# The fourth mixer of a 1-core block stack: compression inputs from two tiles, rotary halves by transfers

## The reference

```python
q = apply_rope(q, cos, sin) * (HEAD_DIM ** -0.5)      # 8 heads of 64, 2 groups
kc, vc, ks, vs, kw, vw = [groups(z) for z in (kc, vc, ks, vs, kw, vw)]   # 2 groups of 64 each
ks = apply_rope(ks, cos, sin)
kw = apply_rope(kw, cos, sin)
k_cmp = apply_rope(compress_blocks(kc, pe_k, w1_k, w2_k), ccos, csin)
v_cmp = compress_blocks(vc, pe_v, w1_v, w2_v)

def apply_rope(x, cos, sin):
    x1, x2 = jnp.split(x, 2, axis=-1)                 # halves of 32 channels
    rot = jnp.concatenate([-x2, x1], axis=-1)
    return x * cos + rot * sin

def compress_blocks(z, pe, w1, w2):                   # 31 blocks of 32 tokens, one every 16 tokens
    blocks = (z[:, :, idx] + pe).reshape(B, G, n_cmp, CMP_BLOCK * d)     # 2048 inputs a block
    return jax.nn.gelu(blocks @ w1) @ w2
```

## Time and profile before

| | |
|---|---|
| median of 3 runs | 2870.78 us (2868.59 to 2872.48) |
| profiled execution | 2868.78 us, its span 2867.0 us |
| mean granted TensorE clock | 0.963 |
| PE, DVE, ACT, POOL busy | 94%, 53%, 34%, 12% of the span |
| stage 7, from gates to the last attention step | about 2085 to 2450 us |

### The profile page before, as it was taken

One profiled execution on the slowest core, in us unless ns is written; L12 is line 12 of the kernel. 1 busy time (PEld: TensorE's weight loads), 2 busy tenths in 40 slices (PEclk: granted clock), 3 DMA queues, 4 the chain that ended last, 5 costly groups with the idle time before them and its releaser, 6 DMA issues.

```text
span 2867.0 us, 32354 instructions
## 1 busy us (share of the span) xinstructions
PE 2704.0 (94%) x13312; PEld 2142.0 (75%) x13312; DVE 1509.2 (53%) x2062; ACT 986.6 (34%) x1662; POOL 350.5 (12%) x306
## 2 busy tenths in 40 slices
PE   7879998999999988899999999999999977999998
PEld 6767876788888665586788888888878534788886
DVE  7965897544334678546434334343365367543333
ACT  3214654422222533543322223222233335332221
POOL 0001001222200001000222102221000000122200
PEclk9979999999999998799999999999999878999999
DMA  3333112122232221001333332223322200133232
GB/s 137 76 83 127 62 53 70 65 98 99 97 96 93 74 67 47 8 2 61 102 99 100 96 98 94 96 96 100 98 92 96 68 15 1 52 104 100 98 94 83
DMA packets 77539, 229.04 MB, mean 80 GB/s; under 512 B 16976, under 2 KB 18256, under 8 KB 77136
## 3 DMA queue, kind: packets, MB, share of 16 engines
q1 hardware_dynamic: 64464, 213.51, 22.9%
q0 software_dynamic: 1840, 5.77, 1.1%
q10 hardware_dynamic: 11088, 7.70, 0.9%
HBM read 221.18 MB, written 5.77 MB: 79 GB/s over the span
## 4 chain that ended last, share of the span: by engine, by line
PE 79%; DVE 13%; ACT 5%; issue 1%; DMA 1%; ACTq 1%; POOL 0%; DVEq 0%; POOLq 0%
PE ps L354 78%; DVE mem L371 5%; DVE part L441 2%; ACT part L429 1%; PE ps L365 1%; DVE mem L384 1%; DMA mem<-lag_dram 1%; DVE mem L2887 1%; DVE mem L377 1%; DVE ps L371 1%; ACTq L1139 1%; DVE mem L389 1%; DVE mem L549 0%; ACT mem L505 0%; DVE mem L630 0%
## 5 line engine op out<-in xcount | busy, mean ns | idle before, releaser
L354 PE MATMUL ps<-part,part 128*128 128x512 f32 (+2 forms) x9918 | 2277.4, 391 | 41.3 <-DVE part L441 18.2
L354 PEld LDWEIGHTS ps<-part,part 128*128 128x128 f32 x9918 | 1855.1, 189 | 461.1 <-DVE part L441 22.0
L441 DVE TENSOR_TENSOR part<-mem,part 128x1024 fp32r<-128x1024 f32 (+2 forms) x421 | 561.2, 1340 | 579.6 <-ACT part L429 579.1
L429 ACT ACTIVATE part<-mem 128x1024 fp32r<-128x1024 f32 (+2 forms) x421 | 417.5, 1002 | 224.6 <-DMA mem<-in_ffb_down 56.7
L371 DVE TENSOR_TENSOR mem<-ps,mem 128x512 f32<-128x512 f32 (+2 forms) x296 | 195.6, 661 | 345.3 <-PE ps L354 335.7
L354 PE MATMUL ps<-mem 128*64 128x64 f32 (+13 forms) x2568 | 273.1, 317 | 60.3 <-DVE mem L371 29.3
L354 PEld LDWEIGHTS ps<-mem 128*64 128x64 f32 (+4 forms) x2568 | 185.3, 169 | 138.8 <-issue 54.5
L513 POOL TENSOR_TENSOR mem<-mem 128x512 f32<-128x512 f32 x62 | 80.8, 1304 | 1132.5 <-ACT mem L505 1131.5
L1557 ACT ACTIVATE part<-mem 128x512 fp32r<-128x512 f32 x88 | 55.6, 632 | 328.5 <-DVE mem L371 328.5
L371 DVE TENSOR_TENSOR mem<-mem 128x512 f32<-128x512 f32 (+10 forms) x289 | 141.8, 491 | 43.2 <-ACT mem L1584 11.4
L1554 ACT ACTIVATE mem<-mem 128x512 f32<-128x512 f32 x88 | 55.6, 632 | 314.2 <-DVE mem L371 314.2
(11 more groups left out here) (178 smaller groups left out, 1060.8 us busy)
## 6 DMA issues: line engine op xcount, KB each, us to landing
mem<-in_ffa_gate SPq DMA_DIRECT2D x44, 512.0 KB, 3.2
mem<-in_ffa_up SPq DMA_DIRECT2D x44, 512.0 KB, 3.2
mem<-in_ffb_gate SPq DMA_DIRECT2D x44, 512.0 KB, 3.2
mem<-in_ffb_up SPq DMA_DIRECT2D x44, 512.0 KB, 3.2
mem<-in_ffa_down SPq DMA_DIRECT2D x32, 512.0 KB, 3.5
mem<-in_ffb_down SPq DMA_DIRECT2D x32, 512.0 KB, 3.6
mem<-in_w_odd SPq DMA_DIRECT2D x24, 512.0 KB, 3.2
mem<-in_w_ab SPq DMA_DIRECT2D x22, 512.0 KB, 3.2
```

Of the source, the lines that this page charges most:

```text
L354: return e.matmul(out, l, r, start=start, stop=stop, skip_group_check=True)
L429: w.e.activation(K.wts[c % NH].h[:, 0:n], K.raws[c % NR][:, 0:n], ACT.Copy).then_inc(*K_A.up(("w", c)))
L441: w.e.tensor_tensor(t.l, K.raws[c % NR][:, 0:n], t.hf, SUB).then_inc(*K.V.up(("w", c)))
```

## The change

The weights hold kc and vc once (two "blocks" tiles, two groups of 64 channels each), so all later weight numbers fall by two. DVE scales each tile from PSUM into SBUF (`E.kv`). POOL issues two transfers that put its halves the other way about into `E.vk`, copies four pieces from `E.kv` into KCX or VCX, waits for the transfers and copies four from `E.vk`. ACT's casts and DVE's subtractions of the two inputs move into the first two rounds.

For cq and ck no product is made. POOL waits for ACT's copy of the tile and issues four transfers of 32 partitions into `turned` (the buffer that held the product before). DVE multiplies the tile by cos, waits for the transfers, multiplies by sin (the sign is in the table now) and adds; it does so one round later, after the next round's first `weights_lo`. The rotation of the compressed keys (`kcm`) and of the third mixer stays a product, with the sign in the table.

```diff
-    rows("w_cd", range(6, 10))
+    rows("w_cd", range(6, 8))
...
+def turn_gpsimd(K, w, name, o, raw, turned, which):
+    w.wait_ge(*K.A[name, o])
+    for r in range(4):
+        a = 32 * (r ^ 1)
+        w.e.dma_start(turned[32 * r:32 * r + 32, :], raw[a:a + 32, 0:T]).then_inc(
+            *K.counts[f"turned{which}"].up((name, o), by=16))
...
+def turned_vector(K, w, name, o, dst, raw, turned, which, cos, sin):
+    w.wait_ge(*K.A[name, o])
+    w.e.tensor_tensor(dst, raw[:, 0:T], cos, MUL).then_inc(*K.V.up())
+    w.wait_ge(*K.counts[f"turned{which}"][name, o])
+    w.e.tensor_tensor(turned, turned, sin, MUL).then_inc(*K.V.up())
+    tt(w, dst, dst, turned, ADD, (name, "rope", o))
...
 (cd_tensor)
-    for _ in linear(K, w, "blocks", 4, 8, K.h, h_ready, K.V):
+    for _ in linear(K, w, "blocks", 2, 8, K.h, h_ready, K.V):
...
         compress_tensor(K, w, i // 4, i % 4)
-        if i < 4:
-            rope_tensor(K, w, "cq", i, E.rope[i % 2][0], T)
-        elif i < 6:
-            rope_tensor(K, w, "ck", i - 4, E.rope[i % 2][0], T)
...
 (cd_vector)
+    for o in range(2):
         weights_lo(K, w, c + 13 + o + 3)
         w.wait_ge(*K.P["blocks", o])
+        w.e.tensor_tensor(E.kv[o], K.acc("blocks", o), K.rstd, MUL).then_inc(*K.V.up(("blocks", o)))
     for o in range(6):
+        weights_lo(K, w, c + 15 + 2 * o + 3)
+        if o < 2:
+            z = (E.KCX, E.VCX)[o]
+            w.wait_ge(*K.A["CX", o])
+            tt(w, E.CX[o].l, z.rearrange("p j n -> p (j n)"), E.CX[o].hf, SUB, ("CX", o))
         if o == 4:
             compress_vector(K, w, 0)
+        if o == 5:
+            cd_keys_vector(K, w)
+        if o:
+            cd_rope_vector(K, w, o - 1)
+        weights_lo(K, w, c + 15 + 2 * o + 4)
+    cd_rope_vector(K, w, 5)
+    weights_lo(K, w, c + 35)
...
 (cd_scalar)
     for o in range(6):
+        weights_hi(K, w, c + 15 + 2 * o + 3)
+        if o < 2:
+            z = (E.KCX, E.VCX)[o]
+            w.wait_ge(*K.G["blocks", o])
+            e.activation(E.CX[o].h, z.rearrange("p j n -> p (j n)"), ACT.Copy).then_inc(*K.A.up(("CX", o)))
...
 (cd_gpsimd)
+    for o in range(2):
+        blocks_gpsimd(K, w, o)
+    for o in range(6):
+        turn_gpsimd(K, w, "cq" if o < 4 else "ck", o % 4, *E.rope[o % 2], o % 2)
...
+def blocks_gpsimd(K, w, o):
+    E, e = K.cd, w.e
+    z = (E.KCX, E.VCX)[o]
+    w.wait_ge(*K.V["blocks", o])
+    landed = K.counts[f"other{o}"]
+    for half in range(2):
+        e.dma_start(E.vk[o][64 * half:64 * half + 64, :], E.kv[o][64 - 64 * half:128 - 64 * half, :]).then_inc(
+            *landed.up("landed", by=16))
+    for other in range(2):
+        if other:
+            w.wait_ge(*landed["landed"])
+        src = (E.kv, E.vk)[other][o].rearrange("p (n s) -> p s n", s=16)
+        for half in range(2):
+            r, g = slice(64 * half, 64 * half + 64), half ^ other
+            for lo in range(2):
+                copy(w, z[r, 8 * lo:8 * lo + 8, 31 * g:31 * g + 31], src[r, half:16:2, lo:lo + 31], ("blocks", o))
```

More of the change, by code:

```diff
@@ L171, in __init__ @@
         inputs = ("consts", "consts1", "params0", "params", "x0", "x1", "x2", "x3", "x4", "x5", "x6", "x7", "ssm_bc", "pool_w", "w2a2", "g2", "nsa_w2")
-        moved = ["raw0", "raw1", "shuffle", "out", "lag_zeros", "lags_out", "lags_in"]
+        moved = ["raw0", "raw1", "shuffle", "turned0", "turned1", "other0", "other1", "out", "lag_zeros", "lags_out", "lags_in"]
         moved += [f"{n}{tl}" for n in ("u_out", "u_in", "y_out", "y_in") for tl in range(4)]
@@ L333, in weight_order @@
     first[7] = len(out)
-    rows("w_cd", [18])
-    rows("w_cd", range(10, 18))
+    rows("w_cd", [16])
+    rows("w_cd", range(8, 16))
     by_token("w_dv", T)
-    rows("w_cd", range(6, 10))
+    rows("w_cd", range(6, 8))
     nsa = [(io["nsa_w1"][kv, c], 1024, False) for kv in range(2) for c in range(4)]
@@ L2473, in __init__ @@
         self.kk = m.tiles(2)
+        self.kv, self.vk = (self.q[:, 2 + k, :] for k in range(2)), (self.kk[:, k, :] for k in range(2))
+        self.kv, self.vk = list(self.kv), list(self.vk)
         self.vt = m.flat(NT * 280).rearrange("p (t c) -> p t c", t=NT)
@@ L2764, in cd_vector @@
     stt(w, E.sin, K.cc("sin"), 0.125, K.rstd, MUL, MUL)
-    turned = K.rstd.rearrange("p (n s) -> p s n", s=16)
-    for o in range(4):
+    for o in range(2):
         weights_lo(K, w, c + 13 + o + 3)
         w.wait_ge(*K.P["blocks", o])
[L2769 to L2778, removed]
-    for o in range(6):
-        weights_lo(K, w, c + 17 + 2 * o + 3)
+        w.e.tensor_tensor(E.kv[o], K.acc("blocks", o), K.rstd, MUL).then_inc(*K.V.up(("blocks", o)))
+    for o in range(6):
+        weights_lo(K, w, c + 15 + 2 * o + 3)
[3 more added lines that the diff above has]
+            tt(w, E.CX[o].l, z.rearrange("p j n -> p (j n)"), E.CX[o].hf, SUB, ("CX", o))
         if o == 4:
             compress_vector(K, w, 0)
[L2783 to L2788, removed]
+        if o == 5:
[5 more added lines that the diff above has]
+    weights_lo(K, w, c + 35)
     w.wait_ge(*K.A["gates_c"])
@@ L2793, in cd_vector, with cd_keys_vector, cd_rope_vector @@
     mlstm_vector(K, w)
-    weights_lo(K, w, c + 39)
+    weights_lo(K, w, c + 37)
     nsa_vector(K, w)
-    out_vector(K, w, 7, lambda o: c + 35 + o, 8, lambda k: K.pc("ffb_norm", 8 + k))
+    out_vector(K, w, 7, lambda o: c + 33 + o, 8, lambda k: K.pc("ffb_norm", 8 + k))
+def cd_keys_vector(K, w):
+    E = K.cd
+    ts(w, E.cos, E.cos, 8.0, None, MUL, None)
+    ts(w, E.sin, E.sin, 8.0, None, MUL, None)
+    w.wait_ge(*K.V.now)
+def cd_rope_vector(K, w, o):
+    E = K.cd
+    name, dst = ("cq", E.q[:, o, :]) if o < 4 else ("ck", E.kk[:, o - 4, :])
+    turned_vector(K, w, name, o % 4, dst, *E.rope[o % 2], o % 2, E.cos, E.sin)
 def compress_vector(K, w, kv):
@@ L2968, in cd_scalar @@
         e.activation(E.dv[:, t, :], K.acc("dv", t), ACT.Copy, scale=K.rT[:, t:t + 1]).then_inc(*K.A.up(("dv", t)))
-    for o in range(4):
+    for o in range(2):
         weights_hi(K, w, c + 13 + o + 3)
[L2971 to L2974, removed]
     for o in range(6):
-        weights_hi(K, w, c + 17 + 2 * o + 3)
+        weights_hi(K, w, c + 15 + 2 * o + 3)
[3 more added lines that the diff above has]
+            e.activation(E.CX[o].h, z.rearrange("p j n -> p (j n)"), ACT.Copy).then_inc(*K.A.up(("CX", o)))
         if o == 4:
@@ L2982, in cd_scalar @@
         rope_scalar(K, w, name, o % 4, E.rope[o % 2][0], T)
-        weights_hi(K, w, c + 17 + 2 * o + 4)
+        weights_hi(K, w, c + 15 + 2 * o + 4)
     for t in range(4):
-        weights_hi(K, w, c + 29 + t + 3)
+        weights_hi(K, w, c + 27 + t + 3)
     for t in range(4):
@@ L2990, in cd_scalar @@
     e.activation(E.gt, E.vt[:, :, 256:280], ACT.Sigmoid).then_inc(*K.A.up("gates_c"))
-    weights_hi(K, w, c + 37)
+    weights_hi(K, w, c + 35)
     compress_scalar(K, w, 1)
     mlstm_scalar(K, w)
-    weights_hi(K, w, c + 39)
+    weights_hi(K, w, c + 37)
     nsa_scalar(K, w)
-    out_scalar(K, w, 7, lambda o: c + 35 + o, 8, lambda k: K.pc("ffb_norm", 8 + k))
+    out_scalar(K, w, 7, lambda o: c + 33 + o, 8, lambda k: K.pc("ffb_norm", 8 + k))
 def compress_scalar(K, w, kv):
@@ L3117, in cd_gpsimd @@
     memset(w, E.kcd, 0.0, "vcm_zeros")
-    out_gpsimd(K, w, 7, lambda o: K.first[7] + 35 + o, 8)
+    for o in range(2):
+        blocks_gpsimd(K, w, o)
+    for o in range(6):
+        turn_gpsimd(K, w, "cq" if o < 4 else "ck", o % 4, *E.rope[o % 2], o % 2)
+    out_gpsimd(K, w, 7, lambda o: K.first[7] + 33 + o, 8)
+def blocks_gpsimd(K, w, o):
[14 more added lines that the diff above has]
+                copy(w, z[r, 8 * lo:8 * lo + 8, 31 * g:31 * g + 31], src[r, half:16:2, lo:lo + 31], ("blocks", o))
 def sync(K, e):
@@ L3227, in _constants @@
         for d in range(32):
-            R[b + d + 32, b + d] = -1
+            R[b + d + 32, b + d] = 1
             R[b + d, b + d + 32] = 1
@@ L3234, in tabs @@
         ang = pos.astype(f)[None, :] * np.tile(inv, 4)[:, None]
-        return np.cos(ang), np.sin(ang)
+        return np.cos(ang), np.sin(ang) * np.where(i % 64 < 32, -1, 1)[:, None]
     a, b = tabs(np.arange(T))
@@ L3351, in _layout @@
     di, df, dog = cd[:, 2328:2332], cd[:, 2332:2336], cd[:, 2336:2848]
-    dup = [np.concatenate([z[:, 64 * g:64 * g + 64]] * 2, 1) for z in (kc, vc) for g in range(2)]
     ifg = np.zeros((1024, P), f)
@@ L3355, in _layout @@
     ifg[:, 32:36] = df
-    out["w_cd"] = _w(np.concatenate([qc, ks, kw] + dup + [dq, dk, dog, ifg], 1))
+    out["w_cd"] = _w(np.concatenate([qc, ks, kw, kc, vc, dq, dk, dog, ifg], 1))
     out["w_cv"] = np.ascontiguousarray(np.concatenate([vs, vw, cg], 1)).reshape(8, P, 280)
```

## The result

The changed kernel took 2856.72 us (median of 5 runs, 2856.34 to 2862.55); the kernel before, run beside it, 2872.48 (median of 5, 2868.59 to 2879.63). The ratio is 0.9948, with a 95% interval of 0.9936 to 0.9960: faster by 0.4 to 0.6%. The forecast was 2855.1 with a range of 2849.5 to 2863. The execution that was profiled is the slowest of the five, 2862.55 (span 2860.7, mean granted clock 0.959), so its end is not the place to read the gain. I read it between points that both traces have: an eviction, the end of a product.

What follows compares the result with a forecast made beforehand. PE's gapless stretch in the fourth mixer was taken as the bound: 16.3 us removed, 0.6 waited, 0 for rotary transfers and clock, so 15.7 gained and 2855.1 us forecast; 8-in-10 range 2849.5 to 2863.

Steps and rivals of the forecast that it cites:

- PE bounds, gapless: Around the fourth mixer, PE alone is the chain from 2129.63 to 2263.86, so PE work removed there shortens the kernel equally.
- Blocks products, 10.9: Two of the four blocks products leave PE, 2 x 5.45 = 10.9 us.
- B: The end of blocks product 0, at 2168.05 in the trace before; the first input's chain is counted from it.
- Rotations, 0.9 each: Six products with the rotation matrix leave PE's rounds, 0.9 us each, 5.4 us together (3.2 to 6.6).
- The input's chain and its wait, 0.6: Scaling, transfers, eight copies, cast and subtraction delay the first compression input; PE waits 0.6 us, ends 0 and 4.5.
- x: Time in us from one of POOL's strided copies to the next; 0.73 taken first, 0.89 for the wait of 0.6.
- the formula: PE's wait ahead of the first compression chunk is 8x - 6.5 us where above zero, x being the time per copy.
- Subtractions that hold copies: Rival: DVE subtractions hold POOL copies for their whole length, 3.1 us wait at the first chunk, 2857.6 us; chance 0.10.
- Rotary transfers hidden, margin 0.9: Transferred rotary halves arrive in time; narrowest at ck 1, before the third cv piece, margin 0.9 us, cost nothing (ends 0, 2).
- The clock, 0 within 3: PE's clock fall behind the mixer piece may shift in time; counted as 0, with 3 us allowed either way.
- POOL as the bound: Slower rival: two waits sum to 16x - 16.2, reaching the 16.3 removed at x = 2.03; chance 0.05.
- second wait: PE waits for the weights of compression chunk 2, by 8x - 9.7 us, beginning at x = 1.21.

Runs made afterwards that it cites:

- copies_free: Changed kernel with DVE's subtraction for the cq 1 weights moved behind the key inputs' own; 2853.16 us in a single run, 2851.88 us when run five times.
- blocks_only: Changed kernel with only the compression half kept (two blocks products, POOL transfers and copies), rotary halves by matrix product as before; 2862.75 us, ratio 0.9964.
- late_last: Changed kernel with three 128x512 copies on POOL ahead of ck 1's transfers, to use up the margin at the third cv piece; 2854.03 us, single run.
- after: First profiled execution of the changed kernel itself, the slowest of its five runs; 2862.55 us.
- repeat: The changed kernel run again without edits; 2858.85 us, ratio 0.9955 to the kernel before.
- rotary_only: Changed kernel with only the rotary half kept (transfers for rotation products), four blocks products written by DVE as before; 2869.70 us, ratio 0.9989.
- copies_twice: Changed kernel with each of POOL's sixteen copies made twice; 2863.41 us, ratio 0.9970 to the kernel before.
- cv_last: copies_free with the four cv pieces moved behind the last two compression chunks; 2855.73 us, ratio 0.9947 to the kernel before.
- all_three: copies_free with cv moved behind the last chunks and the third mixer's rotation products replaced by transfers; 2856.32 us, ratio 0.9941 to the kernel before.

## Why the prediction was right, and where its terms were off

- **PE bounds, gapless.** Right. Every microsecond taken from PE up to cv's eviction was one there: 10.9 + 6 x 0.86 - 0.7 = 15.4, measured 15.5.
- **Blocks products, 10.9.** Right: from B to cq 0's eviction before 21.76, after 10.87 us.
- **Rotations, 0.9 each.** 0.86, the value of the form ahead of the small column sums; the 1.10 of the record was no price. 5.2 for 5.4.
- **The input's chain and its wait, 0.6.** PE stood for 0.42 and the round was 0.7 longer (8.81, the next ones 8.13). The size was right, the reason only in part, and so the size is partly luck: the 0.6 came from x = 0.89, and with the measured x = 0.79 the formula gives no wait. The fixed part was 0.4 too small. The first copy began at B+2.1 where B+1.9 was worked out, and DVE's subtraction for the input took 1.59 in place of 1.23 beside the copies of block 1. The first copy's extra 0.65 never came: it took 0.65, and the others that met nothing 0.60 to 0.65; the 0.87 of the earlier trace rows belongs to another form. The narrow windows of the trace show seven of the eight copies at that length, and one that is not: at 2178.14, beside DVE's subtraction of 2177.95, one took 1.50. x was 0.68 in copies_free, where none was held.
- **Subtractions that hold copies.** This rival, given 0.10 inside the forecast, is the mechanism that was there: one copy in eight, not two, held for 0.9. In block 1 three more took 1.43 to 1.49, and DVE's 1.22 became 1.59. The held copy ended at 2179.64; DVE's subtraction, with two inputs in SBUF, ended at 2179.17, and 0.61 from there is 2179.78. By the rule of the Trainium skill ("SBUF — State Buffer", "Who interferes with whom") the second blocks fully; the trace agrees within 0.14. A copy in blocks_only that met a DVE instruction of 0.69 agrees as well: it took 1.01 and ended 0.47 after it, as this one did. DVE's scaling at 2177.35, one input in PSUM and one in SBUF, held nothing: the copy beside it took 0.63. copies_free takes the meeting away and the wait is gone, which shows it. The two DVE instructions at the held copy, and the input's subtraction:

```profile
2177.35 0.69 DVE L2784 TENSOR_TENSOR mem<-ps,mem 128x512 f32<-128x512 f32 x1 [3.62 <-PE ps L354]
2177.95 1.22 DVE L441 TENSOR_TENSOR part<-mem,part 128x1024 fp32r<-128x1024 f32 x1
2181.43 1.59 DVE L371 TENSOR_TENSOR part<-mem,part 128x1024 fp32r<-128x1024 f32 x1 [2.26 <-ACT part L3001]
```
- **Rotary transfers hidden, margin 0.9.** Right. ck 1's rotary part ended 7.3 us after its eviction (7.1 was worked out) and late_last measured a margin of 0.7. An issue took 0.49 us in place of 0.79, so the fourth began 1.5 after the first and not 2.4; but it landed 3.5 later and not 2.6. The two errors cancel: 5.0 from the first issue (2225.07) to the landing that releases the second operation here (DVE in order of time):

```profile
2226.03 0.68 DVE L1608 TENSOR_TENSOR mem<-mem 128x512 f32<-128x512 f32 x1
2230.06 0.69 DVE L1610 TENSOR_TENSOR mem<-mem 128x512 f32<-128x512 f32 x1 [3.35 <-DMA mem<-mem]
2230.79 0.69 DVE L371 TENSOR_TENSOR mem<-mem 128x512 f32<-128x512 f32 x1
```

- **The clock, 0 within 3.** This is the term that was mis-sized, by 1.45. The clock fell 4.3 us after cv's eviction began before and in blocks_only (returning at 21.3), and 2.7 after it in after, repeat and rotary_only (returning at about 23.1). Here the same order of work gave the same place within 0.1 us. The forecast allowed for this and could not give its sign.
- **POOL as the bound.** Break-even was at x = 2.03; with x = 1.46 copies_twice was still faster than before. The formula for the first wait gave 5.2 and 5.76 were measured. Its second wait was wrong: what came was 4.2 of half clock. Up to cq 2's eviction copies_twice lost 10.3 us to its first input, the 0.7 of the changed kernel included, but 2.4 came back: some 7.8 in the stage, where 16x - 16.2 gives 7.2. The sum of the two waits came out near, by other terms.
- **Sum.** 15.7 forecast; 16.05 removed, 0.7 waited, 1.45 to the clock make 13.9. Stage 7 shows 14.2 (repeat), the medians 15.8 and 14.0. That the first pair of medians gives just the 15.7 of the forecast is luck; the traces and the second pair say some 14. The lower end of the range was 2849.5, where its own terms give 2850.3; nothing hangs on it.

Open: what puts a program's clock where it falls. Behind cv its place came again within 0.1 us in both pairs of executions of one program (the changed kernel and copies_free), and it moved when rotations were taken out, when 0.42 us of idle PE was taken away (copies_free) and when 1.44 was added (late_last). In attention it did not come again: 0.83 and 0.86 on average with one program. The runs give no rule by which cv_last or all_three could have been foreseen.

## What to carry to other kernels

Where the chain of waits is one gapless piece of PE, price what is taken from it by the stretch between two evictions, not by records; then look at the clock behind it, since part of the gain can be given back there, and an idle PE costs its wait and, where the wait is long, the slower matmuls after it. Moving products that only rearrange data to transfers on an idle queue can pay if the taker stands a round behind in its queue: here 5.2 us in the rounds, of which 1.5 went to the clock. When copies on POOL are on the chain, keep DVE's two-input subtractions away from them: one line moved took away 0.7 of wait, and by the clock behind it stage 7 was 3.2 us shorter.

## What the runs showed of the hardware

- A strided copy on POOL of 64 partitions x 8 x 31 elements, every sixteenth element read, took 0.61 us. When it met a DVE instruction with two SBUF inputs that had begun first, it ended 0.47 us after it: 1.50 beside a subtraction of 1.22, 1.01 beside a product of 0.69 (blocks_only). DVE was held by copies in the same way, 1.22 becoming 1.51 to 1.63 (after, copies_free). Three 128x512 copies took 0.61, 1.07 and 0.96 us (late_last).
- Four transfers of 32 partitions x 2 KB within SBUF were issued 0.49 us apart. Where DVE waited for them, the last landed 3.7 us after the first issue (cq 0) and 5.0 (ck 1), 4.3 in late_last for ck 1.
- PE idle for 5.76 us brought 1.2 GHz, which lasted for the next 8.9 us though it worked without a gap again (copies_twice); idle for 0.42 us brought nothing (clock 1.00 from 2183 to 2191).
- The attention stage took 133.9 to 134.6 us in eight profiles and 136.8 to 138.4 in four, with the same instructions; the changed kernel alone gave 137.1 and 134.2. One profile can't judge a change of less than some 3 us in what stands ahead of it.
- The clock can fall to 0.50 while PE works without a gap: in cv_last it did so during three chunks of narrow matmuls (128x64) in a row.
